# An MoE layer's first and last expert pass: rows by selection matmuls, the router on the unscaled residual

## The chip, the cores and the metric

The kernel runs on one core of one Trainium2 chip. The metric is the time on the device in microseconds (us) for one execution, from three runs. A profile of one execution shows its instructions by engine: TensorE (PE, with the weight loads as PEld), VectorE (DVE), ScalarE (ACT), GpSimd (POOL) and SyncE (SP), and the DMA transfers.

## The reference

A trunk of two layers on 256 tokens of width 1024, all in fp32. Layer 0 is attention with sinks and a dense feed-forward of 3584. Layer 1 is a Mamba2 mixer, then a mixture of eight experts of 3584, two per token. The part that the change touches is the end:

```python
h = h + mix                                   # the mixer's output
hn = rmsnorm(h, ln_ffn[1])
logits = hn @ w_router                        # 256 x 8
top_v, top_i = top_k(logits, 2)
gates = softmax(top_v)
for e in range(8):
    h = h + combine[:, e] * (silu(hn @ w_gate[e]) * (hn @ w_up[e])) @ w_down[e]
return rmsnorm(h, ln_final)
```

`rmsnorm` divides each token's row by the root of its mean square and multiplies by a gain.

## The kernel before

Everything lies in one program with an order written out by hand for each engine, and semaphores between them. Tokens stand in two tiles (`TT` = 2) of 128 partitions: `h` is the residual, `xs` a scratch of the same shape. PSUM is eight banks of 512 columns.

**Weights.** They stream as chunks of 1 MB (128x2048) through a ring of six (`ring`, loaded by SP). For precision every product of the large matrices is made of three matmuls: ScalarE rounds a chunk to `w_hi` (L533 in the expert passes), VectorE computes the rest `w_lo` (L1243), and `product` (L604 to L606) multiplies high by high, high by low and low by high. Three chunks can be split ahead (`SPLIT`); `ahead_e` does it for the chunks that it names, ScalarE once TensorE has used the chunk three before (`chunk_used`), VectorE once `hi_ready` says so. SP refills a ring slot once `lo_ready` counts its chunk.

**Before the passes.** The mixer's out product (L604 to L606 on `yT`) ends; VectorE adds it to `h` (L1251). `norm(3, 24)` follows: ScalarE squares (L377), VectorE and ScalarE make the inverse root (L944 to L954), VectorE scales into `xs` (L962), TensorE transposes (L625), VectorE applies the gain into `hT` (L966), and TensorE makes the router's logits, 16 matmuls with `hT` as weights and eight columns of `rw` (L863). VectorE ranks the logits of each token (L1261 to L1276), TensorE counts how many earlier tokens chose each expert (L869 to L873), VectorE makes gates and slots (up to L1310). A slot is a row of `xg_rows` in HBM: 128 rows for each expert, and 128 more where an expert has over 128 tokens. GpSimd scatters the scaled rows there by four indirect DMAs (L348), ScalarE loads the first expert's 128 rows into `xg` (L554), TensorE transposes them (L882), and ScalarE and VectorE split them into `xgT_hi` (L550) and `xgT_lo` (L1319).

**The passes.** A hardware loop (`Fori`) runs `passes` times, 8 with these inputs, over one expert's 42 chunks: gate and up in `WIDE` = 2, 2, 2, 1 groups of 512 columns (28 chunks; the groups start at chunks 0, 8, 16, 24), then down (14 chunks). The number comes into each engine's register by `value_load`. After a group TensorE transposes the hidden rows (L897), which ScalarE and VectorE split (L562, L1328). Towards the end of gate and up TensorE transposes the next expert's rows. The output, 128 rows in banks 6 and 7, is copied to `yg` (L589) and stored to `y_rows` (L591).

**The tail.** GpSimd waits for all stores and gathers each token's two output rows by four indirect DMAs (L359); VectorE adds them to `h` with the gates (L1361), squares (L1364), makes the inverse root and the scaling (L1370), and SP stores `out` (L302).

What sets the order around the change: each engine's instructions run in the order of its program, so a wait holds all that is behind it on that engine.

## Time and profile before

| | |
|---|---|
| median of 3 runs | 1725.51 us (1725.06 to 1726.12) |
| the profiled execution's own time | 1725.92 us |
| its span, first to last instruction | 1724.2 us |
| mean granted TensorE clock | 0.950 |
| TensorE matmuls busy | 1559.2 us (90%) |
| VectorE busy | 1241.1 us (72%) |
| ScalarE busy | 1043.2 us (61%) |
| GpSimd busy | 43.8 us (3%) |
| TensorE's share of the chain that ended last | 67% |

The span is what the sums below are made against. A busy share is an average over the whole kernel; what a change of one stage is worth is read from the timeline of that stage and from the chain of waits, which is followed back from the last instruction, at each step to what released it. Matmuls are pipelined: a row's length (0.39 us) is longer than the step to the next row (0.23 us), and it is the step that adds up.

### The profile page before, as it was taken

The page shows a single profiled execution, that of the slowest core. Times are in us where ns is not written, and L with a number is a line of the kernel's source. Part 1 is how long each engine was busy: PE and PEld are TensorE (multiplying, and loading weights), DVE is VectorE, ACT ScalarE, POOL GpSimd, SP SyncE. Part 2 cuts the span into 40 slices and gives each one's busy share as a digit, 9 for nine tenths or more (in the row PEclk, how much of TensorE's full clock was granted, in tenths as well). Part 3 has the DMA queues.
Part 4 walks back from the last instruction along what each step waited for, and adds up shares of the span by engine and source line. Part 5 has one row for each costly group of instructions (what it writes and reads, how often), then busy time and mean ns, then how long its engine had stood idle before and what let it go on. Part 6 is the DMA issues. An engine that isn't in the chain of part 4 may idle for free.

```text
span 1724.2 us, 21094 instructions
## 1 busy us (share of the span) xinstructions
PE 1559.2 (90%) x7794; PEld 1304.3 (76%) x7794; DVE 1241.1 (72%) x1045; ACT 1043.2 (61%) x886; POOL 43.8 (3%) x90
## 2 busy tenths in 40 slices
PE   5688999989999895699999999999999999999992
PEld 3566888878899785578778778788777777777781
DVE  4554555445498845488888888788888887887885
ACT  4243444334477642476777777777777777777762
POOL 1004200000000001000000000000000000000000
PEclk8888999998999886799999999999999999999996
DMA  7325955544542332699999999999999999999995
GB/s 247 103 74 202 412 199 187 191 150 147 147 123 98 123 110 81 234 353 371 368 359 375 361 367 370 373 346 381 358 356 387 355 354 386 363 358 374 365 366 193
DMA packets 166402, 477.08 MB, mean 277 GB/s; under 512 B 9105, under 2 KB 34977, under 8 KB 166354
## 3 DMA queue, kind: packets, MB, share of 16 engines
q1 hardware_dynamic: 157682, 446.84, 71.3%
q0 software_dynamic: 5520, 18.05, 2.8%
q10 hardware_dynamic: 3152, 11.54, 1.7%
q8 instruction: 32, 0.52, 0.1%
q14 instruction: 16, 0.13, 0.0%
HBM read 455.42 MB, written 20.97 MB: 276 GB/s over the span
## 4 chain that ended last, share of the span: by engine, by line
PE 67%; DVE 15%; issue 8%; ACT 7%; DMA 2%; DVEq 1%; ACTq 0%; POOL 0%; SPq 0%; POOLq 0%
PE bank L604 21%; PE bank L606 20%; PE bank L605 20%; DVE w_lo L1243 7%; ACT w_hi L533 2%; PE bank L897 1%; DVE acc L1174 1%; DVE w_lo L988 1%; DVE m_hT_lo L1328 1%; ACT m_hT_hi L562 1%; DVE arg L1198 1%; ACT w_hi L392 1%; DVE xgT_lo L1319 1%; DMA ring<-swa_w_qkv_in 1%; PE bank L831 1%
## 5 line engine op out<-in xcount | busy, mean ns | idle before, releaser
L1243 DVE TENSOR_TENSOR w_lo<-ring,w_hi 128x2048 fp32r<-128x2048 f32 x339 | 766.8, 2289 | 117.8 <-ACT w_hi L533 117.8
L533 ACT ACTIVATE w_hi<-ring 128x2048 fp32r<-128x2048 f32 x339 | 648.2, 1919 | 255.9 <-PE bank L606 255.6
L604 PE MATMUL bank<-w_hi,xgT_hi 128*128 128x512 f32 x896 | 355.8, 397 | 23.2 <-DVE w_lo L1243 21.7
L606 PE MATMUL bank<-w_hi,xgT_lo 128*128 128x512 f32 x896 | 350.1, 391 | 0.0
L605 PE MATMUL bank<-w_lo,xgT_hi 128*128 128x512 f32 x896 | 349.9, 391 | 0.0
L988 DVE TENSOR_TENSOR w_lo<-ring,w_hi 128x2048 fp32r<-128x2048 f32 (+1 forms) x84 | 190.0, 2266 | 172.2 <-ACT w_hi L392 171.9
L392 ACT ACTIVATE w_hi<-ring 128x2048 fp32r<-128x2048 f32 (+1 forms) x84 | 159.2, 1898 | 171.9 <-PE bank L606 170.3
L604 PEld LDWEIGHTS bank<-w_hi,xgT_hi 128*128 128x128 f32 x896 | 168.9, 188 | 70.1 <-DVE w_lo L1243 34.8
L606 PEld LDWEIGHTS bank<-w_hi,xgT_lo 128*128 128x128 f32 x896 | 168.8, 188 | 35.9
L605 PEld LDWEIGHTS bank<-w_lo,xgT_hi 128*128 128x128 f32 x896 | 169.1, 189 | 33.4
L604 PE MATMUL bank<-w_hi,m_hT_hi 128*128 128x512 f32 x448 | 176.9, 395 | 3.2 <-DVE w_lo L1243 3.2
L606 PE MATMUL bank<-w_hi,m_hT_lo 128*128 128x512 f32 x448 | 174.6, 390 | 0.0
L605 PE MATMUL bank<-w_lo,m_hT_hi 128*128 128x512 f32 x448 | 174.4, 389 | 0.0
L604 PE MATMUL bank<-w_hi,hT_hi 128*128 128x512 f32 (+1 forms) x336 | 133.1, 396 | 2.9 <-DVE hT_lo L978 2.9
L605 PE MATMUL bank<-w_lo,hT_hi 128*128 128x512 f32 (+1 forms) x336 | 131.6, 392 | 0.0
L606 PE MATMUL bank<-w_hi,hT_lo 128*128 128x512 f32 (+1 forms) x336 | 131.3, 391 | 0.0
L604 PEld LDWEIGHTS bank<-w_hi,m_hT_hi 128*128 128x128 f32 x448 | 84.1, 188 | 23.6 <-DVE w_lo L1243 6.6
L606 PEld LDWEIGHTS bank<-w_hi,m_hT_lo 128*128 128x128 f32 x448 | 84.1, 188 | 17.9
L605 PEld LDWEIGHTS bank<-w_lo,m_hT_hi 128*128 128x128 f32 x448 | 84.2, 188 | 16.5
L604 PEld LDWEIGHTS bank<-w_hi,hT_hi 128*128 128x128 f32 x336 | 64.8, 193 | 18.6 <-DVE hT_lo L978 3.3
L604 PE MATMUL bank<-hT_hi,w_hi 128*128 128x256 f32 x256 | 73.3, 286 | 3.1 <-DVE w_lo L988 1.6
L606 PEld LDWEIGHTS bank<-w_hi,hT_lo 128*128 128x128 f32 x336 | 64.7, 193 | 13.3
(260 smaller groups left out, 1692.1 us busy)
## 6 DMA issues: line engine op xcount, KB each, us to landing
ring<-moe_w_gu_in SPq DMA_DIRECT2D x230, 1024.0 KB, 7.4
ring<-moe_w_down_in SPq DMA_DIRECT2D x112, 1024.0 KB, 7.4
ring<-ffn_w_gu_in SPq DMA_DIRECT2D x28, 1024.0 KB, 5.0
ring<-ffn_w_down_in SPq DMA_DIRECT2D x14, 1024.0 KB, 4.8
xg_rows<-zeros POOLq DMA_DIRECT2D x36, 256.0 KB, 12.5
ring<-ssm_w_in_in SPq DMA_DIRECT2D x8, 1024.0 KB, 4.9
ring<-ssm_w_in_in SPq DMA_DIRECT2D x16, 512.0 KB, 3.8
ring<-ssm_w_in_in SPq DMA_DIRECT2D x32, 256.0 KB, 4.2
```

What stands on the lines that cost most here:

```text
L392: act.activation(w_hi[:, m % SPLIT, 0:w], ring[:, m % RING, 0:w], ACT.Copy).then_inc(hi_ready, 1)
L533: act.activation(w_hi[:, c % SPLIT], ring[:, c % RING], ACT.Copy).then_inc(hi_ready, 1)
L562: act.activation(m_hT_hi[:, 4 * f:4 * f + 4, :], bank[4 + f % 2][:].rearrange("p (a b) -> p a b", b=P), ACT.Copy).then_inc(m_This, 1)
L604: pe.matmul(o, stat[0], mov[0], start=start, stop=False)
L605: pe.matmul(o, stat[0], mov[1], start=False, stop=False)
L606: return pe.matmul(o, stat[1], mov[0], start=False, stop=stop)
L831: ins = pe.matmul(bank[4 + t][:, r * P:(r + 1) * P], dtA[:, t, g * REP + r:g * REP + r + 1].to_broadcast([P, P]), tri[:], start=True, stop ...
L897: ins = pe.transpose(bank[4 + f % 2][:, a * P:(a + 1) * P], m_hh[:, f % 2, a * P:(a + 1) * P], ident[:])
L988: dve.tensor_tensor(w_lo[:, m % SPLIT, 0:w], ring[:, m % RING, 0:w], w_hi[:, m % SPLIT, 0:w].bitcast(F32), ALU.subtract).then_inc(lo_ready, 1)
L1174: ins = dve.scalar_tensor_tensor(acc[:, i], U[:, i, tap:tap + T], cwT[:, tap, ct:ct + 1], acc[:, i], ALU.mult, ALU.add)
L1198: ins = dve.tensor_scalar(arg[:, t, r], bank[4 + t][:, r * P:(r + 1) * P], acol[:, t * SH + g * REP + r:t * SH + g * REP + r + 1], 0.0, AL ...
L1243: dve.tensor_tensor(w_lo[:, c % SPLIT], ring[:, c % RING], w_hi[:, c % SPLIT].bitcast(F32), ALU.subtract).then_inc(lo_ready, 1)
```

## The change

- **Router on the unscaled residual.** The router's weights are multiplied once, early, by the norm's gain (`rwg_ready`). TensorE transposes `h` itself as each half is added; ScalarE copies (`raw_T`); the logits come transposed (8 x 256, `rw` as weights), are copied by ScalarE and transposed back. The ranking needs no scaling. The inverse root `inv` is made from squares on VectorE and used from the selection on; the exponent takes the scaled difference of logits.
- **Residual adds.** Tile 0 of the last out product is finished first, and its adds wait for that alone (`so_first`).
- **Pass 0's rows.** VectorE makes a 128x128 selection for each token tile, one where token and slot of expert 0 meet, times `inv`; 16 fp32 matmuls of `h` by it give the transposed rows in eight PSUM places (`first_rows`); ScalarE and VectorE split them with the gain. Scatter and HBM rows remain for the other passes, and the scatter's preparation (slots, scaled rows `xs`) stands behind that split on VectorE; ScalarE's wait for `rows_ready` is still ahead of its passes. The load of `xg` for the next pass stands in the third group of a pass.
- **Last pass.** The loop runs `last` = passes - 1 times and the last pass is written out behind it. In it VectorE makes the gates (`shares`) and the last expert's selection matrix, gathers for the other outputs run into `xs` (choice 0, then choice 1 once those are added), and VectorE adds them (`rows_added`).
- **Tail.** The last pass's output is not stored; four fp32 matmuls of 512 columns bring its rows back to their tokens, weighted; VectorE adds, ScalarE squares by halves, and `out` is stored in two halves.

```diff
+        first_rows = [bank[b][:, P * a:P * (a + 1)] for b, a in FIRST_AT]
+        sel_first, logits_T = m_sg[:, 0, 0:T].rearrange("p (t s) -> p t s", t=TT), m_sg[0:E, 1, 0:T]
...
+            for t in range(TT):
+                sp.wait_ge(out_ready, t + 1)
+                sp.dma_start(out[0, t * P:(t + 1) * P], xs[:, t]).then_inc(out_stored, 16)
+            sp.wait_ge(out_stored, 16 * TT)
 
 
...
                 pool_e.sem_inc(y_free, 1)
-            for t in range(TT):
-                for i in range(2):
-                    pool_e.indirect_dma_start(y_got[:, i, t], None, y_rows.rearrange("i p d -> (i p) d"),
+
+            for i in range(2):
+                if i == 1:
+                    pool_e.wait_ge(y_added, TT)
+                for t in range(TT):
+                    pool_e.indirect_dma_start(xs[:, t], None, y_rows.rearrange("i p d -> (i p) d"),
                                               bass.IndirectOffsetOnAxis(slots_i[:, i, t:t + 1], 0)
...
+            for i in range(4):
+                act.wait_ge(xT_mm, 12 + i + 1)
+                part = (slice(None), slice((i % 2) * 4, (i % 2) * 4 + 4), slice((i // 2) * P, (i // 2 + 1) * P))
+                act.activation(hT[part], bank[4 + i][:].rearrange("p (a b) -> p a b", b=P), ACT.Copy).then_inc(raw_T, 1)
+            act.wait_ge(var_done, 4)
+            act.activation(st[:, 3, 4:6], st[:, 3, 2:4], ACT.Sqrt).then_inc(sqrt_done, 1)
+            act.wait_ge(r_mm, 1)
+            act.activation(logits_T, bank[0][0:E, 0:T], ACT.Copy).then_inc(r_sb, 1)
+            for k in range(KD):
+                act.wait_ge(first_mm, (1, 1, 2, 2, 3, 3, 4, 5)[k])
+                act.activation(xgT_hi[:, k], first_rows[k], ACT.Copy,
+                               scale=vT[:, 24 + k:25 + k]).then_inc(first_hi, 1)
+            ahead_e(0, 2, AHEAD)
             act.wait_ge(r_max, 1)
             act.activation(rt[:, 2], rt[:, 1], ACT.Exp).then_inc(r_exp, 1)
             act.wait_ge(rows_ready, TT)
             act.dma_start(gain_row, ln_final.partition_broadcast(P)).then_inc(gain_loaded, 16)
-            ahead_e(0, 2, AHEAD)
             act.wait_ge(r_passes, 1)
-            passes = act.value_load(passes_i[0:1, 0:1], min_val=E, max_val=2 * E)
-
-            def rows_split(at):
...
+                    act.activation(sel_last_T, bank[0][:, 0:T].rearrange("p (t s) -> p t s", t=TT), ACT.Copy
+                                   ).then_inc(last_sb, 1)
+                else:
...
+                    load_roots(4)
+                    act.wait_ge(m_y, it + 1)
+                    act.wait_ge(y_free, it + 1)
+                    act.activation(yg[:, 0:512], bank[6][:], ACT.Copy).then_inc(y_left, 1)
+                    return
...
-                act.wait_ge(slot_loaded[r], passes * (LAYER_CHUNKS // RING * 16) + (slot_base[r] + 16))
-            act.wait_ge(xg_loaded, passes * 16 + 32)
-            load_roots(4)
+
+            with act.Fori(0, last) as it:
+                expert(it, False)
+            expert(last, True)
+            for n in range(2):
+                for t in range(TT):
+                    act.wait_ge(h_final, 2 * n + t + 1)
+                    act.activation(xs[:, t, 512 * n:512 * (n + 1)], h[:, t, 512 * n:512 * (n + 1)], ACT.Square,
+                                   accum_out=rt[:, 12, 2 * n + t:2 * n + t + 1]).then_inc(sq_final, 1)
+            for r in range(RING):
+                act.wait_ge(slot_loaded[r], last * (LAYER_CHUNKS // RING * 16)
+                            + (slot_base[r] + LAYER_CHUNKS // RING * 16 + 16))
             act.wait_ge(var_done, 5)
...
+            out_product(7, (0,)).then_inc(so_first, 1)
+            out_product(7, (1,))
+
+
...
+                    if k % 4 == 0:
+                        pe.wait_ge(h_done, 8 + 2 * t + k // 4 + 1)
+                    ins = pe.transpose(bank[4 + 2 * t + k // 4][:, (k % 4) * P:(k % 4 + 1) * P],
+                                       h[:, t, k * P:(k + 1) * P], ident[:])
+                    if k % 4 == 3:
+                        ins.then_inc(xT_mm, 1)
+            pe.wait_ge(rwg_ready, 1)
+            for t in range(TT):
+                for k in range(KD):
+                    if k % 4 == 0:
+                        pe.wait_ge(raw_T, 2 * t + k // 4 + 1)
+                    ins = pe.matmul(bank[0][0:E, t * P:(t + 1) * P], rw[:, k, :], hT[:, k, t * P:(t + 1) * P],
                                     start=(k == 0), stop=(k == KD - 1))
+            ins.then_inc(r_mm, 1)
+            pe.wait_ge(r_sb, 1)
+            for t in range(TT):
+                ins = pe.transpose(bank[0][:, T + t * E:T + (t + 1) * E], logits_T[:, t * P:(t + 1) * P],
+                                   ident[0:E, 0:E])
             ins.then_inc(r_logit, 1)
             pe.wait_ge(r_sel, 1)
             chosen = rt[:, 5].rearrange("p (t e) -> p t e", t=TT)
 
             pe.matmul(bank[1][:, 0:E], tri_lt[:], chosen[:, 0, :], start=True, stop=True)
             pe.matmul(bank[1][:, E:2 * E], ones[:], chosen[:, 0, :], start=True, stop=False)
...
-            pe.matmul(bank[1][:, 2 * E:3 * E], ones[:], chosen[:, 0, :], start=True, stop=False)
-            pe.matmul(bank[1][:, 2 * E:3 * E], ones[:], chosen[:, 1, :], start=False, stop=True).then_inc(r_cnt, 1)
+            pe.matmul(bank[1][:, E:2 * E], tri_lt[:], chosen[:, 1, :], start=False, stop=True).then_inc(r_cnt, 1)
...
+
+            pe.wait_ge(sel_ready, 1)
+            for k in range(KD):
+                for t in range(TT):
+                    ins = pe.matmul(first_rows[k], h[:, t, k * P:(k + 1) * P], sel_first[:, t],
+                                    start=(t == 0), stop=(t == TT - 1))
+                if FIRST_AT[k] not in ((2, 0), (3, 0), (4, 0)):
+                    ins.then_inc(first_mm, 1)
             pe.wait_ge(r_passes, 1)
-            passes = pe.value_load(passes_i[0:1, 0:1], min_val=E, max_val=2 * E)
-
-
-            def rows_transposed(at):
-
-                pe.wait_ge(xg_loaded, at * 16 + 16)
+            last = pe.value_load(last_i[0:1, 0:1], min_val=E - 1, max_val=2 * E - 1)
...
                             m_transposes(2 * j - 1)
                 pe.wait_ge(m_silu, it * NJ + NJ)
-                rows_transposed(it + 1)
+                if is_last:
+                    pe.wait_ge(last_ready, 1)
+                    for t in range(TT):
+                        ins = pe.transpose(bank[0][:, t * P:(t + 1) * P], sel_last[:, t], ident[:])
+                    ins.then_inc(last_T, 1)
+                else:
+                    rows_transposed(it)
...
+            with pe.Fori(0, last) as it:
+                expert(it, False)
+            expert(last, True)
+
+            pe.wait_ge(last_sb, 1)
+            for n in range(2):
+                pe.wait_ge((y_left, y_right)[n], 1)
+                for t in range(TT):
+                    pe.matmul(bank[2 * n + t][:], sel_last_T[:, t], yg[:, 512 * n:512 * (n + 1)], start=True,
+                              stop=True).then_inc(back_mm, 1)
...
+            for t in range(TT):
+                dve.wait_ge(*((so_first, 1), (chunk_used, SO0 + KI // 2))[t])
                 for n in range(2):
...
+            dve.drain()
+            for t in range(TT):
+                dve.scalar_tensor_tensor(xs[:, t], h[:, t], 1.0, h[:, t], ALU.mult, ALU.mult,
+                                         accum_out=st[:, 3, t:t + 1])
+            dve.drain()
+            variance(D, st[:, 3], var_done)
...
+            inv = inverse(st[:, 3], sqrt_done, 4)
+            dve.tensor_reduce(rt[:, 7, 0:TT], r3[0], AXX, ALU.max)
+
+            place = bank[1][:, 0:2 * E].rearrange("p (t e) -> p t e", t=TT)
+            dve.wait_ge(column_ready, 1)
+            dve.wait_ge(r_cnt, 1)
+            dve.scalar_tensor_tensor(rt[:, 11, 0:TT], r3[5][:, :, 0], -FAR, place[:, :, 0], ALU.mult, ALU.add)
+            dve.drain()
+            for t in range(TT):
+                ins = dve.tensor_scalar(sel_first[:, t], column, rt[:, 11, t:t + 1], inv[:, t:t + 1], ALU.is_equal,
+                                        ALU.mult)
+            ins.then_inc(sel_ready, 1)
+            dve.wait_ge(r_cnt, 2)
+            dve.tensor_reduce(rt[:, 9, 0:1], bank[0][:, 0:E], AXX, ALU.max)
+            dve.tensor_scalar(r3[6], place, P - 0.5, float((E - 1) * P), ALU.is_gt, ALU.mult)
+            dve.drain()
+            dve.tensor_scalar(rt[:, 9, 1:2], rt[:, 9, 0:1], P + 0.5, float(E), ALU.is_gt, ALU.mult)
+            dve.tensor_tensor(r3[6], r3[6], first_slot[:], ALU.add)
+            dve.drain()
+            dve.tensor_scalar(last_i[:], rt[:, 9, 1:2], float(E - 1), None, ALU.add).then_inc(r_passes, 1)
+            dve.tensor_tensor(r3[6], r3[6], place, ALU.add)
+
+
+            for k in range(KD):
+                dve.wait_ge(first_hi, (2, 2, 4, 4, 6, 6, 7, 8)[k])
+                ins = dve.scalar_tensor_tensor(xgT_lo[:, k], first_rows[k], vT[:, 24 + k:25 + k],
+                                               xgT_hi[:, k].bitcast(F32), ALU.mult, ALU.subtract)
+                if k % 4 == 3:
+                    ins.then_inc(xg_lo, 1)
+            ahead_e(0, 2, AHEAD)
...
+            dve.tensor_tensor(r3[1], r3[0], rt[:, 7, 0:TT].unsqueeze(2).to_broadcast([P, TT, E]), ALU.subtract)
...
+            dve.drain()
+            dve.tensor_tensor(r3[1], r3[1], inv.unsqueeze(2).to_broadcast([P, TT, E]), ALU.mult).then_inc(r_max, 1)
             dve.tensor_tensor(by_choice[:], choice[:], r3[6].unsqueeze(1).to_broadcast([P, 2, TT, E]), ALU.mult)
             dve.drain()
             dve.tensor_reduce(slots[:], by_choice[:], AXX, ALU.add)
             dve.drain()
             dve.tensor_copy(slots_i[:], slots[:]).then_inc(r_slots, 1)
-            ahead_e(0, 2, AHEAD)
+            dve.wait_ge(ffn_gain_loaded, 16)
+            for t in range(TT):
+                dve.scalar_tensor_tensor(xs[:, t], h[:, t], inv[:, t:t + 1], gain_row, ALU.mult,
+                                         ALU.mult).then_inc(rows_ready, 1)
...
+            def shares():
+
+                dve.wait_ge(r_exp, 1)
...
+                for t in range(TT):
+                    ins = dve.tensor_scalar(sel_last[:, t], column, rt[:, 14, t:t + 1], rt[:, 13, t:t + 1],
+                                            ALU.is_equal, ALU.mult)
+                ins.then_inc(last_ready, 1)
+
+            def rows_added(i, t):
+
+                dve.wait_ge(y_got_in, 16 * TT * (i + 1))
+                dve.scalar_tensor_tensor(h[:, t], xs[:, t], gates[:, i, t:t + 1], h[:, t], ALU.mult,
+                                         ALU.add).then_inc(y_added, 1)
...
+                    if is_last and j == 0:
+                        shares()
+                    if is_last and j == 2:
+                        rows_added(0, 0)
+                    ahead_e(it, up + 3, up + wide + 3)
+                    if is_last and j == 2:
+                        rows_added(0, 1)
+                    ahead_e(it, up + wide + 3, up + 2 * wide + 3)
...
-                rows_split(it + 1)
+                if not is_last:
+                    rows_split(it)
...
+                ahead_e(it, c + 4, c + 6)
+                if is_last:
+                    rows_added(1, 0)
+                ahead_e(it, c + 6, c + 8)
+                if is_last:
+                    rows_added(1, 1)
+                ahead_e(it, c + 8, LAYER_CHUNKS)
+                if not is_last:
+                    ahead_e(it + 1, 0, AHEAD)
+
+            with dve.Fori(0, last) as it:
+                expert(it, False)
+            expert(last, True)
+            dve.wait_ge(chunk_used, last * LAYER_CHUNKS + (MOE0 + LAYER_CHUNKS))
+            dve.tensor_copy(yg[:, 512:1024], bank[7][:]).then_inc(y_right, 1)
+            for n in range(2):
                 for t in range(TT):
-                    dve.wait_ge(y_got_in, 16 * 2 * TT)
-                    dve.scalar_tensor_tensor(h[:, t], y_got[:, i, t], gates[:, i, t:t + 1], h[:, t], ALU.mult, ALU.add)
-                dve.drain()
-            for t in range(TT):
-                dve.scalar_tensor_tensor(xs[:, t], h[:, t], 1.0, h[:, t], ALU.mult, ALU.mult,
-                                         accum_out=st[:, 4, t:t + 1])
+                    dve.wait_ge(back_mm, 2 * n + t + 1)
+                    hh = h[:, t, 512 * n:512 * (n + 1)]
+                    dve.tensor_tensor(hh, hh, bank[2 * n + t][:], ALU.add).then_inc(h_final, 1)
+            dve.wait_ge(sq_final, 4)
+            dve.tensor_tensor(st[:, 4, 0:2], rt[:, 12, 0:2], rt[:, 12, 2:4], ALU.add)
```

## Rows read from the trace of the kernel before

**Rows 1.** Timeline: start and length in us, engine, line, operation; before the passes.
```profile
654.78 2.29 DVE L1243 TENSOR_TENSOR w_lo<-ring,w_hi 128x2048 fp32r<-128x2048 f32 x1 [2.47 <-ACT w_hi L533]
...
657.78 0.39 PE L606 MATMUL bank<-w_hi,yT_lo 128*128 128x512 f32 x1
658.21 2.73 DVE L1251 SCALAR_TENSOR_TENSOR h<-bank,st,h 128x512 f32<-128x512 f32 x4 [1.14 <-PE bank L606]
...
669.05 7.00 PE L863 MATMUL bank<-rw,hT 128*128 128x8 f32 x32 [0.78 <-DVE hT L966]
...
678.07 0.18 DVE L1276 TENSOR_SCALAR rt<-rt 128x16 f32<-128x16 f32 x1
...
705.09 0.79 PE L604 MATMUL bank<-w_hi,xgT_hi 128*128 128x512 f32 x1 [1.49 <-DVE xgT_lo L1319]
```

**Rows 2.** Chain of waits: start and length in us, what; passes 0 and 1.
```profile
688.24 10.11 DMA xg_rows<-xs,slots_i
...
705.88 0.43 PE bank L605
...
727.45 0.50 PE bank L604
727.95 0.23 PE bank L605
...
918.49 1.29 DVE xgT_lo L1319 x2
```

**Rows 3.** Timeline of the end of the last pass and the tail.
```profile
1691.24 0.39 PE L606 MATMUL bank<-w_hi,m_hT_lo 128*128 128x512 f32 x1
...
1708.08 5.04 DVE L1361 SCALAR_TENSOR_TENSOR h<-y_got,gates,h 128x1024 f32<-128x1024 f32 x4 [12.18 <-DMA y_got<-y_rows,slots_i]
...
1715.68 0.17 DVE L944 TENSOR_SCALAR st<-st 128x2 f32<-128x2 f32 x1
...
1717.32 2.48 DVE L1370 SCALAR_TENSOR_TENSOR xs<-h,st,gain_row 128x1024 f32<-128x1024 f32 x2
1719.83 0.39 SPq L302 DMA_DIRECT2D out<-xs  x1
```

**Rows 4.** Timelines of TensorE, VectorE and ScalarE, start of pass 1.
```profile
839.11 0.50 PE L604 MATMUL bank<-w_hi,xgT_hi 128*128 128x512 f32 x1 [1.41 <-DVE w_lo L1243]
...
850.68 0.50 PE L604 MATMUL bank<-w_hi,xgT_hi 128*128 128x512 f32 x1 [0.38 <-DVE w_lo L1243]
...
848.34 6.70 DVE L1243 TENSOR_TENSOR w_lo<-ring,w_hi 128x2048 fp32r<-128x2048 f32 x3 [1.91 <-ACT w_hi L533]
...
844.12 1.28 ACT L572 ACT_TABLE_LOAD   x1
```

**Rows 5.** Timeline of TensorE in the scan stage: fp32 matmuls.
```profile
545.61 2.00 PE L831 MATMUL bank<-tri,dts 128*128 128x128 f32 x16
...
547.89 0.60 PE L844 MATMUL bank<-xs 128*128 128x256 f32 x2
548.33 0.38 PE L845 MATMUL bank<-xs 128*128 128x128 f32 x2
```

**Rows 6.** Stretches: busy us and count per engine, PEclk, DMA share, GB/s.
```profile
658.00:664.00 6.00, 0.17 (x1) 0.00 (x0) 3.93 (x11) 3.78 (x6) 0.00 (x0) 0.92 0.00 0
...
850.00:973.00 123.00, 119.73 (x541) 97.92 (x540) 104.12 (x59) 91.12 (x63) 0.00 (x0) 1.00 0.99 366
```

**Rows 7.** Source line 544: instructions, ns min/median/max, first and last start.
```profile
L544 ACTq TENSOR_LOAD <-passes_i x1: 469/469/469, 681.5 to 681.5; - x1
```

**Rows 8.** The page, part 5: groups, busy us, mean ns, idle before.
```profile
L1243 DVE TENSOR_TENSOR w_lo<-ring,w_hi 128x2048 fp32r<-128x2048 f32 x339 | 766.8, 2289 | 117.8 <-ACT w_hi L533 117.8
L533 ACT ACTIVATE w_hi<-ring 128x2048 fp32r<-128x2048 f32 x339 | 648.2, 1919 | 255.9 <-PE bank L606 255.6
```

**Rows 9.** Source lines 338 and 348: the DMA issues of POOL, ns.
```profile
L338 POOL DMA_DIRECT2D xg_rows<-zeros x36: 542/543/584, 153.5 to 172.2; - x36
...
L348 POOL DMA_INDIRECT xg_rows<-xs,slots_i x4: 955/975/2189, 683.2 to 688.2; - x4
```

131 lines of the change are left out of this document (64 added, 67 removed).

## The prediction

> **What bounds the kernel now.** I read the page's chain first: most of it is TensorE in the split matmuls of the expert passes, which run one behind the other. The change does not touch these, nor the splitting of the weights. So I looked for where TensorE stands still around them, and two stretches come out. In the timeline of the stretch before the passes, the out product's last matmul starts at 657.78 and ends 0.39 later, at 658.17, and the first matmul of pass 0 starts at 705.09 [rows 1]: 46.9 us. The chain of waits fills them: 2.7 of residual adds, squares, a root, transposes, 7.0 of router matmuls, the ranking, then the scatter (10.11 from its last issue to landing) and the load of `xg` [rows 1, 2]. After the last matmul, which starts at 1691.24 and ends at 1691.6, come 32.6 us to the end of the span at 1724.2 [rows 3]: the store of `yg`, four gathers, four adds (5.0), squares, root, scaling, the store of `out`. Between them lie eight passes; pass 0 reaches its chunk 7 at 727.45, pass 1 at 850.68 [rows 2, 4], 123.2 us apart. All eight look alike, so a gain in front is worth what it moves the arrival at chunk 7 of pass 0, and a gain behind is worth what it takes off the 32.6.
>
> **The front, up to the first expert matmul.** Z is 658.17.
> Residual adds: 2.73 for four [rows 1]. The first two now wait only for the half product of tile 0, but VectorE is busy with a `w_lo` until 657.07 [rows 1], so they run 657.1 to 658.5 and the others to 659.9: 1.1 us earlier, not 2.7. Transposes of `h` follow each add; with four at 0.5 (four records of 0.125, [rows 5]) they end at 660.4. The norm's root goes off the path: two squares on VectorE of 1.26 each (as an add of that size, [rows 3]) end at 662.4, the root is needed only at the selection. The matmul now has `rw` as weights and 128 token columns, 16 of fp32, 32 records. The nearest rows are 16 records of fp32 128x128 in 2.00 us at full clock [rows 5], and the 32 of the old router in 7.00 at half [rows 1, 6]; so 4.0 or 7.0, less if the eight-column weights load quickly. I take 3.6 (full clock, since TensorE has been nearly continuously busy since Z): 664.0. Then a copy of 256 columns (an estimate from the 0.68 of a 512-column add: 0.4), two transposes and hops, 0.9: 664.9. The ranking took from 676.05, the router's end, to 678.25 [rows 1], with one instruction more: 667.0. Three of five count matmuls at 0.44 (two records of 0.22, [rows 1]) end at 668.4; meanwhile VectorE makes the inverse root (1.2 of the tail's 1.64, [rows 3]) and the maximum, 668.4; offset 0.25 and two 128x128 selections of 0.3 each (an estimate, under half the 0.68 of 512 columns): 669.2.
> The selection: 16 fp32 matmuls, 32 records, 4.0 us at full clock and 7.0 at half [rows 1, 5]. Over 658 to 664 the mean clock was 0.92 with TensorE idle [rows 6]: 1.00 for 5 us, then 0.50, so it fell 4.9 us after Z; here it stands nearly idle from 664.9 to 669.2 with only the counts between. I take mostly half clock with a rise near the end: 6.2, so 675.4. The last `xgT_hi` (estimated 0.35 for 128 columns), the last `xgT_lo` (0.3) and hops are 0.85, and TensorE's own load of `last` costs 0.5 and some registers, about the same [rows 7]. First expert matmul S = 676.4, against 705.09: 28.7 earlier, between 27.5 (all half clock) and 31 (all full).
>
> **What is late next: the scatter's instructions now stand in the first chunks' way.** The pass has three chunks split ahead and needs chunk 3 at S + 8.2 (12 matmuls of 0.227 per chunk, 2.72, at full clock, [rows 2]). Before, VectorE and ScalarE had all else done while the scatter ran. After, VectorE does, behind the last `xgT_lo`: the `w_lo` of chunk 2 (its `w_hi`, 1.92, [rows 8], starts after the last `first_hi`, so S + 1.4 to S + 3.7), some seven small instructions for exponent and slots (1.2), the two scaled rows of 1.2 each: `rows_ready` at S + 7.4. ScalarE waits for `rows_ready` ahead of a DMA issue (0.33), its load of `last` and registers (0.47, and 0.5 estimated, [rows 7]), then the loop's table load (1.28, [rows 4]) and the `w_hi` of chunk 3 (1.92); then `w_lo` (2.29) [rows 8]: S + 14.4. TensorE idles from S + 8.2, 6.2 us. A 4.9 us idle lost the clock after Z [rows 6], so chunk 3 runs at 0.427 per matmul, as pass 0 began before [rows 2]: 2.3 more. From chunk 3 to chunk 7 pass 1 took 11.57, from 839.11 to 850.68, through `w_hi`, a table load, two `silu` and `w_hi` [rows 4]; that chain starts at chunk 3's end. So chunk 7 comes at S + 14.4 + 11.6 + 2.3 = S + 28.3 = 704.7, against 727.45 (S + 22.4 before, [rows 2]). The front's gain at chunk 7 is 22.7: 28.7 earned, 6.0 given back. Ends: 16 if the entry costs twice what I think, 31 if chunk 3 is in time and all is at full clock.
>
> **In the passes.** The scatter runs beside pass 0. POOL's four issues began from 683.2 to 688.2, and the last landed 10.11 later, 15 us after the first began [rows 2, 9]; from S + 8.5 that is S + 24, and the load of `xg` that waits for it stands at ScalarE's third group, past S + 47. Weights use 0.99 of the DMA time at 366 GB/s in a pass [rows 6], but `w_lo` waited for ScalarE alone, in all 117.8 us [rows 8], and while it idles to S + 14.4 nothing asks for chunk 9. Zero. The moved `xg` issue stands where ScalarE's next `w_hi` ends over 1 us before VectorE wants it: zero, at most 0.35 x 7.
> Last pass: the dozen small instructions of `shares` (2.2) fall into VectorE's 1.9 idle before chunk 7's `w_lo` [rows 4]: 0.3. Of four `rows_added` at 1.26 [rows 3], the first stands right on the chain `m_hT_lo`, `w_lo`, TensorE: 1.3, the second 0.3, the two in the down part have 0.4 idle per chunk and 1.1 of lead: 0. Removed are the two `xgT_lo`, together 1.29, from the chain [rows 2] and six transposes (0.7): -1.9. Sum 0, between -2 and +6. The gathers for choice 0 are issued 10 us into the pass and wanted at 47 us; those for choice 1 are issued after the adds and wanted about 40 us later.
>
> **The tail.** T is the last matmul's end, 1691.6. The left half of `yg` is copied 0.6 before T, the right half by VectorE until T + 0.7. Four fp32 matmuls of 512 columns: a 256-column one and its successor are 0.44 apart [rows 5], so 0.88 each, 3.5 in all at full clock; the halves overlap with the adds (0.68 each), last add T + 4.3, last square on ScalarE (0.6 + 0.2) T + 5.1, sum and drain 0.3, then as before from 1715.68 to 1719.80 the root and two scalings, 4.1 [rows 3]: T + 9.6. The `out` store took 4.4 from 1719.83; of its half I take 3.9. T + 13.5 against T + 32.6: 19.1 gained, between 16 (matmuls at half clock) and 20.
>
> **The Trainium skill against this.** POOL's 36 zero-fill issues stood beside VectorE's work of the dense stage, `w_lo` among it, and took 542 to 584 ns each [rows 9]; no blocking shows in them. The Trainium skill, page "SBUF — State Buffer", section "Who interferes with whom" and the box on the "DVE blocks DMA" trap, says GpSimd and VectorE share a port pair that one of them holds exclusively, and descriptors of POOL's DMAs are not written meanwhile; "GPSIMD Engine Reference", "Key points", adds VectorE instructions with two SBUF inputs, which `w_lo` is. This would put the scatter and gathers, which stood in idle stretches, under the lock. By that rule the time is the third rival's below.
>
> **The sum.** 1724.2 - 22.7 - 19.1 + 0 = 1682.4 for the span. The median of the runs (1725.5) is 1.3 above this span, and the profiled run itself 1725.9, 1.7 above: 1684 by the median.
>
> **The rivals.**
> 1. Entry is not late: ScalarE's wait for `rows_ready` or the small instructions are hidden, chunk 3 starts by S + 9, and no clock is lost: 5.5 to 8 less, 1677. For it: only three chunks lie ahead, and I have sized the VectorE queue from single rows. Against: the order is written out, and `rows_ready` is behind 2.3 + 1.2 + 2.4 of it. Chance 0.17.
> 2. Longer hops and half clock all the way through the router too (3.4 more), with a later entry (3 more): 1691. For it: pass 0 began at half clock before [rows 2]. Chance 0.12.
> 3. The change runs its indirect DMAs beside `w_lo`, and each takes VectorE's time: eight issues of 0.97 [rows 9], fully on VectorE's critical stretches, 8 us: 1692. Chance 0.06.
> 4. Slower than before: the gathers of the last pass starve behind the weight stream (0.99 DMA share, [rows 6]). VectorE waits for them in order, with `w_lo` behind it, and so TensorE. The first pair is wanted 37 us after its issue, landing took 10 for the scatter's [rows 2]; from 37 us on, each microsecond counts once, and beyond about 79 us the kernel is slower than before; at 85 us it takes 1732. Against: the scatter landed in 10 while three weight loads were in flight with it. Chance 0.02.
> 5. The change does not do what it says, since the expert loads would fill more than 128 rows and passes exceed 8: excluded by the 339 `w_lo`, 8 x 42 and three ahead [rows 8].
>
> **How the numbers follow.** The forecast, 1684 with its own range 1679 to 1689, has 0.62. The range goes from 1676 (rival 1 with a full-clock front) to 1693 (rival 3), leaving out about 0.15. Measurement tells 0.2% from no change, 3.5 us; every case but rival 4 is faster by ten times that: faster 0.97, same 0.01, slower 0.02.
>
> **What would show it.** First expert matmul 18 us after Z; a TensorE gap of some 6 us before chunk 3 ending in `w_lo`, with ScalarE's table load before it; chunk 7 some 28 us into the pass; passes 123 us apart; the last pass within 2 us of the others; 13.5 us from the last expert matmul to the end. Wrong if the gap before chunk 3 is absent (rival 1) or over 9 us, if `w_lo` grows beyond 2.3 us, or if VectorE waits for a gather.

## The result and the profile after

The changed kernel takes 1681.58 us (median of 4 runs, 1680.24 to 1683.25) against 1725.82 for the kernel before it in the same runs (1725.06 to 1726.12): ratio 0.9745, 95% interval 0.9728 to 0.9762, so 44.2 us less. Its profiled execution has a span of 1681.5 us. The forecast was 1684.

The timeline of the changed kernel from the out product's last matmul to chunk 7 of pass 0 (start and length in us, engine, line, operation; in brackets the idle time before and what ended it); it answers to [rows 1, 2]:

```profile
658.43 2.72 DVE L1344 SCALAR_TENSOR_TENSOR h<-bank,st,h 128x512 f32<-128x512 f32 x4
659.23 0.39 PE L651 MATMUL bank<-w_hi,yT_lo 128*128 128x512 f32 x1
661.79 3.66 PE L919 MATMUL bank<-hT,rw 128*8 128x128 f32 x32
668.15 0.17 DVE L1370 TENSOR_SCALAR rt<-rt 128x16 f32<-128x16 f32 x1
670.18 0.60 DVE L1380 TENSOR_SCALAR m_sg<-trig,rt,st 128x128 f32<-128x128 f32 x2
670.83 5.62 PE L940 MATMUL bank<-m_sg,h 128*128 128x128 f32 x32
677.51 0.49 PE L649 MATMUL bank<-w_hi,xgT_hi 128*128 128x512 f32 x1 [1.06 <-DVE xgT_lo L1396]
...
681.99 2.47 DVE L1415 SCALAR_TENSOR_TENSOR xs<-h,st,gain_row 128x1024 f32<-128x1024 f32 x2
684.49 0.33 ACTq L570 DMA_DIRECT2D gain_row<-ln_final_in  x1
685.91 1.28 ACT L549 ACT_TABLE_LOAD   x1 [4.19 <-issue]
687.21 5.51 ACT L549 ACTIVATE w_hi<-ring 128x2048 fp32r<-128x2048 f32 x3
691.49 0.80 PE L649 MATMUL bank<-w_hi,xgT_hi 128*128 128x512 f32 x1 [5.51 <-DVE w_lo L1336]
```

Z, the end of the out product, is 659.62. The router takes 3.66 on a TensorE that has not rested; ranking and counts come back; the selection runs from 670.83; the first expert matmul is S = 677.51 = Z + 17.9 (before: Z + 46.9). Then comes the price: ScalarE waits for the scaled rows (681.99 to 684.46), issues the load of the gain row, loads `last`, loads a table, and only at 687.21 makes the `w_hi` of chunk 3. TensorE idles 5.51 us and starts chunk 3 at 691.49; chunk 7 follows at 704.70, Z + 45.1 (before: Z + 69.3).

The clock in that stretch (us, then busy time and count of TensorE, its weight loads, VectorE, ScalarE and GpSimd, then PEclk, DMA share, GB/s):

```profile
666.00:668.00 2.00, 0.20 (x2) 0.11 (x2) 1.46 (x6) 0.00 (x0) 0.00 (x0) 0.94 0.00 0
668.00:670.00 2.00, 1.62 (x8) 1.62 (x8) 1.20 (x9) 0.00 (x0) 0.00 (x0) 0.50 0.00 0
...
690.00:694.00 4.00, 2.51 (x6) 2.04 (x7) 4.00 (x3) 2.72 (x2) 2.27 (x1) 0.50 0.65 181
```

The granted clock falls to 0.50 (1.2 GHz) twice: where TensorE waits for the ranking, and in the wait for chunk 3.

The timeline of the last pass and the tail of the changed kernel, answering to [rows 3]:

```profile
1565.78 0.50 PE L649 MATMUL bank<-w_hi,xgT_hi 128*128 128x512 f32 x1 [0.48 <-DVE w_lo L1336]
...
1614.09 0.50 PE L649 MATMUL bank<-w_hi,xgT_hi 128*128 128x512 f32 x1 [1.77 <-DVE w_lo L1336]
...
1668.04 0.60 ACT L619 ACTIVATE yg<-bank 128x512 f32<-128x512 f32 x1 [4.08 <-PE bank L651]
1668.79 3.67 PE L1019 MATMUL bank<-yg,zeros 128*128 128x512 f32 x8
...
1675.93 2.48 DVE L1520 SCALAR_TENSOR_TENSOR xs<-h,st,gain_row 128x1024 f32<-128x1024 f32 x2
1677.24 1.55 SPq L313 DMA_DIRECT2D out<-xs  x2
```

T, the last expert matmul's end, is 1668.69, and the end comes 12.8 us later (before: 32.6).

The changed kernel and all kernels made from it have the same program up to Z (the kernel before lacks the early product of router weights and gain, the new order at the end of the out product and some small preparations), and yet Z lies between 656.5 and 659.6 in their profiles. So I compare traces from Z on. From Z to the end the kernel before takes 1724.2 - 658.17 = 1066.0, the changed one 1021.9: 44.1 less, of it 24.2 up to chunk 7 of pass 0, 0.2 from there to T, 19.8 behind T.

### The profile page after: what moved, and what is told of

Its sections match the earlier page's. It is cut to its first block, busy times and chain, and to the rows that moved or that the text cites. A ratio compares the mean times of both kernels' runs of the same rounds, so it can differ in the third digit from the quotient of the medians.

```text
span 1681.5 us, 21145 instructions
## 1 busy us (share of the span) xinstructions
PE 1562.1 (93%) x7822; PEld 1302.9 (77%) x7822; DVE 1233.8 (73%) x1056; ACT 1037.6 (62%) x894; POOL 56.9 (3%) x93
## 4 chain that ended last, share of the span: by engine, by line
PE 69%; DVE 15%; issue 7%; ACT 7%; DVEq 1%; DMA 1%; ACTq 1%; SPq 0%
PE bank L649 21%; PE bank L651 21%; PE bank L650 20%; DVE w_lo L1336 7%; ACT w_hi L549 2%; PE bank L964 1%; DVE acc L1267 1%; DVE w_lo L1079 1%; DVE m_hT_lo L1459 1%; ACT m_hT_hi L586 1%; DVE arg L1291 1%; ACT w_hi L408 1%; DMA ring<-swa_w_qkv_in 1%; PE bank L877 1%; DVE xgT_lo L1452 1%
## 5 line engine op out<-in xcount | busy, mean ns | idle before, releaser
L1336 DVE TENSOR_TENSOR w_lo<-ring,w_hi 128x2048 fp32r<-128x2048 f32 x336 | 759.6, 2288 | 110.5 <-ACT w_hi L549 110.4
L651 PEld LDWEIGHTS bank<-w_hi,m_hT_lo 128*128 128x128 f32 x448 | 84.1, 188 | 17.9
```

The costliest lines, as they stand in the source:

```text
L651: return pe.matmul(o, stat[1], mov[0], start=False, stop=stop)
L1336: dve.tensor_tensor(w_lo[:, c % SPLIT], ring[:, c % RING], w_hi[:, c % SPLIT].bitcast(F32), ALU.subtract).then_inc(lo_ready, 1)
```

## The experiments

All edits are to the changed kernel. The first three columns are the median, its ratio to the kernel before and the 95% interval; the others, from each profile, are: from Z to the end, to the first expert matmul, to chunk 3 and to chunk 7 of pass 0; from that chunk 7 to T; from T to the end. The rows stem from four sets of runs, each with the kernel before in it (medians 1725.4 to 1725.8); the changed kernel was timed in the first set alone, so small differences between medians are read with the trace beside them.

| kernel | us | ratio | interval | Z to end | S | chunk 3 | chunk 7 | to T | tail |
|---|---|---|---|---|---|---|---|---|---|
| before | 1725.8 | 1 | | 1066.0 | 46.9 | 57.9 | 69.3 | 964.2 | 32.6 |
| changed | 1681.6 | 0.9745 | .9728-.9762 | 1021.9 | 17.9 | 31.9 | 45.1 | 964.0 | 12.8 |
| e6 tail undone | 1697.4 | 0.9838 | .9821-.9854 | 1036.7 | 18.0 | 31.9 | 45.2 | 961.5 | 30.0 |
| e7 router scaled | 1692.3 | 0.9797 | .9776-.9817 | 1031.5 | 26.9 | 41.1 | 54.8 | 963.9 | 12.8 |
| e8 selection undone | 1696.4 | 0.9828 | .9812-.9845 | 1036.1 | 37.4 | 48.0 | 59.4 | 963.9 | 12.8 |
| e1 gain moved | 1678.3 | 0.9730 | .9717-.9743 | 1018.5 | 17.9 | 28.6 | 41.7 | 964.0 | 12.8 |
| e2 exponent early | 1675.4 | 0.9704 | .9691-.9717 | 1014.4 | 18.0 | 26.2 | 37.7 | 963.9 | 12.8 |
| e3 entry clear | 1675.1 | 0.9710 | .9697-.9723 | 1014.5 | 17.9 | 26.2 | 37.7 | 964.0 | 12.8 |
| e4 rows on GpSimd | 1676.1 | 0.9711 | .9698-.9725 | 1016.1 | 19.0 | 27.3 | 39.5 | 963.7 | 12.9 |
| e5 warm | 1681.1 | 0.9743 | .9727-.9760 | 1020.4 | 15.7 | 29.7 | 43.7 | 963.9 | 12.9 |
| e10 small gathers | 1682.0 | 0.9744 | .9730-.9757 | 1021.9 | 17.9 | 31.9 | 45.1 | 964.0 | 12.8 |
| e9 two loads | 1683.4 | 0.9752 | .9739-.9766 | 1024.6 | 17.9 | 31.9 | 45.2 | 966.7 | 12.8 |
| e12 together | 1671.6 | 0.9684 | .9671-.9697 | 1010.9 | 15.7 | 24.0 | 35.5 | 962.6 | 12.8 |
| e13 Silu first | 1666.1 | 0.9651 | .9638-.9664 | 1005.8 | 15.7 | 24.0 | 34.9 | 958.0 | 12.9 |

**Each part undone by itself.** First the tail.

```diff
-                if is_last:
-                    load_roots(4)
...
-                    act.activation(yg[:, 0:512], bank[6][:], ACT.Copy).then_inc(y_left, 1)
-                    return
...
-                    pe.matmul(bank[2 * n + t][:], sel_last_T[:, t], yg[:, 512 * n:512 * (n + 1)], start=True,
-                              stop=True).then_inc(back_mm, 1)
...
+            pool_e.wait_ge(y_stored, last * 16 + 16)
...
+                    pool_e.indirect_dma_start(y_got[:, i, t], None, y_rows.rearrange("i p d -> (i p) d"),
...
+                    dve.scalar_tensor_tensor(h[:, t], y_got[:, i, t], gates[:, i, t:t + 1], h[:, t], ALU.mult, ALU.add)
```

> Edit to the changed kernel: front and written-out last pass stay, but the last pass stores its outputs, all four gathers follow it, and the adds, squares, root and store of out are those of the kernel before. Theory A (the tail's gain is the round trip through DRAM): 32.6 us from the last expert matmul to the end instead of 12.8; the last pass is 0.9 shorter between its chunk 7 and its end since the adds no longer stand in it; the pass ahead of it stays at 121.9 us, since the two table loads of the loop are gone with the writing out, not with the new tail: 1681.6 + 19.8 - 0.9 = 1700.5. Rival B (the 1.3 us of the last pass are the tail's doing): 1701.8. Rival C (the store of yg and the gathers are faster here than before, since fewer loads stand beside them): under 1698.

Measured: 1697.4, 15.9 more, and 14.8 in the trace: 17.2 more behind T, 2.5 less between chunk 7 and T. The tail is 30.0, not 32.6. Theories A and B did not have that; rival C had the time (under 1698), but gave as its cause a faster store and faster gathers. The timeline of the kernel before where `yg` is copied, and below it that of e6, with its first adds:

```profile
1691.67 1.91 ACT L533 ACTIVATE w_hi<-ring 128x2048 fp32r<-128x2048 f32 x1 [0.80 <-PE bank L606]
1693.48 1.07 ACT L589 ACTIVATE yg<-bank 128x512 f32<-128x512 f32 x2
```

```profile
1662.53 1.28 ACT L617 ACTIVATE yg<-bank 128x512 f32<-128x512 f32 x2 [5.56 <-PE bank L638]
...
1676.81 2.48 DVE L1469 SCALAR_TENSOR_TENSOR h<-y_got,gates,h 128x1024 f32<-128x1024 f32 x2 [17.50 <-DMA y_got<-y_rows,slots_i]
```

Before, ScalarE still split a chunk of a next pass that never came, and copied `yg` from T + 1.9; written out, the last pass has no next one, and the copy starts at T - 0.7. From the copy's start to the first add it is 14.6 before and 14.3 in e6, so rival C's cause is worth 0.3 at most. So 2.5 of the tail's 19.8 come from writing the pass out, 17.2 from the matmuls that return its outputs.

Then the router on the normalised rows again:

```diff
+            inv = inverse(st[:, 3], sqrt_done, 4)
+            for t in range(TT):
+                dve.tensor_scalar(xs[:, t, :], h[:, t, :], inv[:, t:t + 1], None, ALU.mult).then_inc(xs_done, 1)
...
-                                       h[:, t, k * P:(k + 1) * P], ident[:])
+                                       xs[:, t, k * P:(k + 1) * P], ident[:])
```

> Edit to the changed kernel: the router sees the normalised rows again (squares, root, scaling, then transposes), the selection matmuls and the tail stay. Theory A (the norm's chain comes onto the path and TensorE idles in it and loses the clock): router starts at Z + 8.0 instead of Z + 2.2, takes 7.0 instead of 3.7, the inverse root after the ranking is gone (0.3 on the path, since the counts take as long): first expert matmul at Z + 26.5 instead of Z + 17.9, 8.6 us more: 1690. Rival B (the clock is not lost in the wait): 3.3 less than that, 1687.

Transposes and router in e7's timeline:

```profile
665.35 3.67 PE L910 MATMUL bank<-ident,xs 128*128 128x128 f32 x16 [6.53 <-DVE xs L1354]
668.95 4.40 PE L919 MATMUL bank<-hT,rw 128*8 128x128 f32 x32
```

TensorE waits 6.53 us for the norm, and transposes and router take 3.67 and 4.40 instead of 2.41 and 3.66. S is 9.0 later and chunk 7 9.7: theory A's total, but not its terms. The router began at Z + 10.1, not Z + 8.0, and ran at half clock for a small part only; transposes and router together lost 2.0 where A had 3.3 for the router alone. The four runs spread from 1686.5 to 1693.2, so the trace is the better measure here.

Pass 0's rows through scatter and gather again:

```diff
-                    ins = pe.matmul(first_rows[k], h[:, t, k * P:(k + 1) * P], sel_first[:, t],
-                                    start=(t == 0), stop=(t == TT - 1))
...
+            act.dma_start(xg, xg_rows[0]).then_inc(rows_back, 16)
...
+            pe.wait_ge(rows_back, 16)
...
+                ins = pe.transpose(bank[k // 4][:, (k % 4) * P:(k % 4 + 1) * P], xg[:, k * P:(k + 1) * P], ident[:])
```

> Edit to the changed kernel: pass 0's rows go through the scatter and a load of xg again, transposed and split as in the kernel before; the router on the unscaled residual and the tail stay. Theory A: slots and scaled rows at Z + 15.8, four scatter issues 5.2, landing about 10, load of xg 2.5, transposes and split 2.5: first expert matmul at Z + 36.5 instead of Z + 17.9; but the entry is clear again (chunk 7 at S + 22.4 instead of S + 27.2), so chunk 7 at Z + 58.9 instead of Z + 45.1: 13.8 us more, 1695.4. Rival B (the late chunk 3 is no property of the selection's short stretch and stays): 18.6 more, 1700.

The transposes of `xg` in e8's timeline:

```profile
692.12 1.97 PE L943 MATMUL bank<-ident,xg 128*128 128x128 f32 x8 [22.90 <-DMA xg<-xg_rows]
```

TensorE waited 22.90 us for that load. S is at Z + 37.4 and chunk 7 at Z + 59.4, so S + 22.0 against S + 27.2 in the changed kernel: theory A. The selection earns 19.5 at S and keeps 14.3 at chunk 7. In the traces the three parts are worth 14.8, 9.6 and 14.2 from Z to the end. What the written-out pass is worth by itself is e6 against the kernel before, from chunk 7 of pass 0 to the end: 991.5 against 996.8, so 5.3. The sum is 43.9 of 44.1. The earlier adds of tile 0, kept in all of these kernels, were not undone by themselves.

**The entry of pass 0.** The three kernels take one thing after another out of the wait for chunk 3. First e1:

```diff
-            act.wait_ge(rows_ready, TT)
-            act.dma_start(gain_row, ln_final.partition_broadcast(P)).then_inc(gain_loaded, 16)
...
+                    if is_last and j == 1:
+                        act.wait_ge(rows_ready, TT)
+                        act.dma_start(gain_row, ln_final.partition_broadcast(P)).then_inc(gain_loaded, 16)
```

> Edit to the changed kernel: ScalarE's wait for rows_ready and the load of the last gain row (the DMA issue behind it) move out of the entry of pass 0 into the written-out last pass. Theory A (ScalarE's wait holds chunk 3 and the long idle costs the clock): the w_hi of chunk 3 starts about 184.4-Z style, that is 24.8 us after the end Z of the out product instead of 27.6, its w_lo ends at Z + 29.0; TensorE idles 2.5 us instead of 5.5, the clock stays up and chunk 3's matmuls take 0.23 instead of 0.43: 3.0 + 2.3 = 5.3 us less, 1676.3. Rival B (VectorE is the late one: its w_lo of chunk 2, small instructions, scaled rows and its load of last fill the same time): idle stays above 4 us, at most 1.5 less, 1680 to 1681.6. Rival C (the clock is lost for another reason than this idle stretch): 3.0 less only, 1678.6.

The `w_hi` of chunk 3 and TensorE's chunk 3 in e1's timeline, and e1's stretch behind:

```profile
681.12 5.51 ACT L549 ACTIVATE w_hi<-ring 128x2048 fp32r<-128x2048 f32 x3
...
685.42 0.69 PE L650 MATMUL bank<-w_hi,xgT_hi 128*128 128x512 f32 x1 [2.19 <-DVE w_lo L1337]
```

```profile
685.00:689.00 4.00, 3.58 (x9) 2.80 (x10) 4.00 (x3) 1.64 (x1) 3.39 (x3) 0.57 0.72 174
```

The wait for `rows_ready` was what held ScalarE: the idle stretch is 2.19 instead of 5.51. But the clock falls all the same, to 0.57 in the mean of 685 to 689: theory A's second half is wrong, and 3.4 is gained, not 5.3. That is rival C's number (1678.6), though e2 shows that the clock does depend on this idle stretch: one of 2.19 us was still long enough to lose it here. Next, e2:

```diff
             act.activation(logits_T, bank[0][0:E, 0:T], ACT.Copy).then_inc(r_sb, 1)
+            act.activation(root_table[:, 4:5], ones[:, 4:5], ACT.Exp)
+            act.wait_ge(r_max, 1)
+            act.activation(rt[:, 2], rt[:, 1], ACT.Exp).then_inc(r_exp, 1)
...
             dve.tensor_tensor(r3[6], r3[6], place, ALU.add)
+            dve.drain()
+            dve.tensor_tensor(r3[1], r3[0], rt[:, 7, 0:TT].unsqueeze(2).to_broadcast([P, TT, E]), ALU.subtract)
...
+            dve.tensor_copy(slots_i[:], slots[:]).then_inc(r_slots, 1)
```

> As e1_gain_moved, and the ranking's small instructions (choice, slots, the exponent's argument) move into VectorE's idle stretch between the offset and the first xgT_lo, ScalarE's Exp and its table load to between the logits' copy and the first xgT_hi. Theory A: VectorE has 1.2 us less ahead of the w_lo of chunk 3 and ScalarE 1.6 + 1.3 less; VectorE is now the one that binds: w_lo of chunk 2 until Z + 21.4, scaled rows 2.5, its load of last about 1, w_lo 2.3: chunk 3 at Z + 27.3, idle 1.2 us, 1.3 to 1.7 less than e1_gain_moved, 1674.8. Rival B (ScalarE waits for r_max longer than its stretch allows, and the xgT_hi start late): S up to 1 us later, no gain over e1_gain_moved, 1676.3 to 1677.

The timelines of ScalarE, VectorE and TensorE in e2:

```profile
678.71 1.28 ACT L549 ACT_TABLE_LOAD   x1
680.58 1.92 ACT L549 ACTIVATE w_hi<-ring 128x2048 fp32r<-128x2048 f32 x1 [0.59 <-PE bank L653]
...
683.33 4.49 DVE L1338 TENSOR_TENSOR w_lo<-ring,w_hi 128x2048 fp32r<-128x2048 f32 x2
...
685.83 0.39 PE L651 MATMUL bank<-w_hi,xgT_hi 128*128 128x512 f32 x1
```

ScalarE is now ready at 680.58, VectorE's `w_lo` ends at 685.6, and TensorE goes on at 685.83 without a gap, at full clock: chunk 7 at Z + 37.7, 7.4 earlier than in the changed kernel and 6.2 less by the medians. With the last 2.2 of idle the clock's loss went too.

e3 moves the loads of `last` as well, and e4 makes the scaled rows on GpSimd:

> As e2_exp_early, and the loads of last on VectorE and ScalarE move into the same idle stretches ahead of the selection's results. Theory A: 1 us less on VectorE's queue ahead of the w_lo of chunk 3: chunk 3 at Z + 26.4, idle 0.3 us, 0.9 less than e2_exp_early, 1673.9. Rival B (the load of last on ScalarE delays the Exp and with it the first xgT_hi): S later by 0.5 to 1 us and the same time as e2_exp_early, 1674.8.

```diff
-                dve.scalar_tensor_tensor(xs[:, t], h[:, t], inv[:, t:t + 1], gain_row, ALU.mult,
-                                         ALU.mult).then_inc(rows_ready, 1)
...
+                pool_e.tensor_scalar(xs[:, t], h[:, t], st[:, 3, 6 + t:7 + t], None, ALU.mult)
...
+                pool_e.tensor_tensor(xs[:, t], xs[:, t], gain_row, ALU.mult).then_inc(rows_ready, 1)
```

> As e3_entry_clear, and the two scaled rows are made by GpSimd (two plain instructions for each instead of VectorE's one). Theory A (VectorE's queue alone still held chunk 3): chunk 3 is in time, no idle stretch ahead of it, 0.3 to 1 us less than e3_entry_clear, 1673.3; the scatter starts later, and nobody waits for it. Rival B (GpSimd's elementwise instructions with two SBUF inputs and VectorE's w_lo or small instructions take turns at the SBUF): w_lo of chunks 2 and 3 or the xgT_lo grow by some tenths to microseconds, and the time is 1 to 5 us longer than e3_entry_clear. Rival C (the scatter ends too late for the load of xg in pass 0): a TensorE idle stretch ahead of the transposes of xg, more than 5 us longer.

e3 equals e2 in the trace, since the entry was clear already: the 0.9 of its theory A did not come. e4 is worse by 1.5 there, 1.0 by the medians. Its timelines show GpSimd's two steps of the scaling, and VectorE's instructions of 16 columns and `w_lo` beside them:

```profile
669.78 5.68 POOL L360 TENSOR_SCALAR xs<-h,st 128x1024 f32<-128x1024 f32 x2 [487.32 <-DVE m_sg L1389]
669.94 0.98 DVE L1397 TENSOR_TENSOR rt<-rt,first_slot 128x16 f32<-128x16 f32 x1
672.75 1.00 DVE L1406 TENSOR_TENSOR rt<-rt,st 128x16 f32<-128x16 f32 x1
...
680.53 6.82 POOL L363 TENSOR_TENSOR xs<-xs,gain_row 128x1024 f32<-128x1024 f32 x2 [5.07 <-issue]
682.46 11.44 DVE L1345 TENSOR_TENSOR w_lo<-ring,w_hi 128x2048 fp32r<-128x2048 f32 x4 [2.27 <-ACT w_hi L556]
```

The first of the two small ones takes 0.17 in e2 and 0.98 here, while GpSimd's scaling runs, and S came 1.1 later. The `w_lo` grow too: of the four in the last row the first takes 2.63 and the second, of chunk 4, 4.32 instead of 2.29, and TensorE waits 0.92 us for it. GpSimd's multiplication by the gain row takes 2.41 and then 4.45, so both sides lose. That is rival B as it was written down.

**The clock in the selection.**

```diff
+            for _ in range(8):
+                pe.matmul(bank[7][:, 0:P], ident[:], hT[:, 0, 0:P], start=True, stop=True)
             pe.wait_ge(r_sel, 1)
...
+            for _ in range(4):
+                pe.matmul(bank[7][:, 0:P], ident[:], hT[:, 0, 0:P], start=True, stop=True)
             pe.wait_ge(sel_ready, 1)
```

> Edit to the changed kernel: 8 fp32 matmuls of 128 columns into a free bank while TensorE waits for the ranking, 4 while it waits for the selection. Theory A (the clock falls because TensorE stands idle for 2.2 us there, and the selection is slow for that alone): the granted clock stays at 1.00 from Z to the first expert matmul, the counts take 0.22 instead of 0.43 each and the selection 4.1 instead of 5.4: first expert matmul at Z + 16.0 instead of Z + 17.9, 1.9 us less, 1679.7. Rival B (the counts of 8 columns are no work that holds the clock, and it falls in them): up to 0.6 less, 1681. Rival C (the extra matmuls end later than the ranking and stand in the way): 0.5 to 1 us more.

Stretches of e5, and below them the selection in its timeline:

```profile
666.00:668.00 2.00, 1.80 (x16) 1.61 (x16) 1.48 (x10) 0.00 (x0) 0.00 (x0) 1.00 0.00 0
...
690.00:694.00 4.00, 4.00 (x12) 3.12 (x11) 2.01 (x1) 0.81 (x1) 0.00 (x0) 0.56 0.95 347
```

```profile
668.85 3.76 PE L944 MATMUL bank<-m_sg,h 128*128 128x128 f32 x32
```

The clock stays at 1.00 up to S, the selection takes 3.76 instead of 5.62, S is 2.2 earlier: theory A up to there. But the 5.5 us of idle ahead of chunk 3 stay, TensorE starts again at 687.67 and the clock is back only about 693.5, so chunk 3 takes 5.3 instead of 4.5. Chunk 7 is 1.4 earlier, and the medians, 0.5 apart, do not resolve it.

**GpSimd beside VectorE.** 24 more gathers of 8 KB beside the `w_lo` of pass 0:

```diff
+            for c in range(10, 34):
+                pool_e.wait_ge(hi_ready, MOE0 + c + 1)
+                pool_e.indirect_dma_start(zeros[:, 16 * (c - 10):16 * (c - 9)], None, xg_rows.rearrange("i p (a d) -> (i p a) d", d=16),
```

> Edit to the changed kernel: GpSimd issues 24 more indirect gathers of 128 rows of 64 bytes (8 KB each, so hardly any traffic) beside the w_lo of pass 0, each paced by a w_hi. Theory A (GpSimd waits for VectorE and not the other way round): GpSimd's issues take 2 to 5 us beside w_lo instead of 0.95 alone, w_lo stays within 0.1 of 2.29, and the time is the same, up to 0.5 more: 1681.6 to 1682.1. Rival B (each issue takes VectorE's time, as my third rival had it): 24 x 0.95, 23 us more at most and at least 10, w_lo of pass 0 near 3.2: 1692 to 1705.

Timelines of GpSimd and VectorE and the page's group of `w_lo` in e10:

```profile
710.15 3.08 POOL L368 DMA_INDIRECT zeros<-xg_rows,slots_i  x1 [0.30 <-issue]
...
717.58 2.29 DVE L1343 TENSOR_TENSOR w_lo<-ring,w_hi 128x2048 fp32r<-128x2048 f32 x1 [0.42 <-ACT w_hi L556]
718.27 2.42 POOL L368 DMA_INDIRECT zeros<-xg_rows,slots_i  x1 [0.30 <-issue]
...
733.64 4.60 DVE L1343 TENSOR_TENSOR w_lo<-ring,w_hi 128x2048 fp32r<-128x2048 f32 x2
733.65 0.95 POOL L368 DMA_INDIRECT zeros<-xg_rows,slots_i  x1 [0.30 <-issue]
```

```profile
L1343 DVE TENSOR_TENSOR w_lo<-ring,w_hi 128x2048 fp32r<-128x2048 f32 x336 | 759.7, 2288 | 110.4 <-ACT w_hi L556 110.3
```

The issues take 0.94 to 3.08 us, `w_lo` stays at 2288 ns in the mean, and time and trace are the changed kernel's (1021.9 from Z both): theory A. The rows show how: each of the 18 issues that began while a `w_lo` was under way ended 0.8 to 0.9 us after the end of that `w_lo` (718.27 + 2.42 against 717.58 + 2.29), so one that began early in it took long. Two began within 0.01 us of a `w_lo`'s start (733.65 is one); they took 0.95, and that `w_lo` 2.33. No `w_lo` took over 2.35, and the four issues that met none took 0.94 or 0.95. So GpSimd waits for VectorE here, and nobody waits for GpSimd.

**The table loads of the last pass.** (`load_roots` is one Sqrt of one column.) In the last pass chunk 3 has no gap, and chunk 7 comes 1565.78 - 1443.90 = 121.9 after that of pass 6, against 123.2 before. The row of pass 6:

```profile
1443.90 0.50 PE L649 MATMUL bank<-w_hi,xgT_hi 128*128 128x512 f32 x1 [0.38 <-DVE w_lo L1336]
```

```diff
             def expert(it, is_last):
+                if is_last:
+                    load_roots(4)
```

> Edit to the changed kernel: one Sqrt of one column at the start of the written-out last pass, so that this pass has the two table loads that the loop body has. Theory A (the last pass is 1.3 us shorter from chunk 7 to chunk 7 only because straight-line code keeps the Silu table): a TensorE gap of 1.35 to 1.55 ahead of chunk 3 of the last pass, chunk 7 to chunk 7 is 123.2 instead of 121.9, 1.3 more: 1682.9. Rival B (the last pass is shorter since the registers and branches of the loop are gone): 121.9 stays and the time is 1681.6.

Timelines of ScalarE and TensorE at the start of e9's last pass:

```profile
1547.21 1.28 ACT L386 ACT_TABLE_LOAD   x1 [0.68 <-ACT yg L629]
...
1552.90 0.50 PE L652 MATMUL bank<-w_hi,xgT_hi 128*128 128x512 f32 x1 [1.12 <-DVE w_lo L1339]
1564.60 0.50 PE L652 MATMUL bank<-w_hi,xgT_hi 128*128 128x512 f32 x1 [0.48 <-DVE w_lo L1339]
```

The gap ahead of chunk 3 is back (1.12), and chunk 7 to chunk 7 is 123.2 again: theory A. The medians differ by 1.8. The trace has 2.7 more, since another 1.3 went after the gap of 1.77 at the adds: in e9 the clock fell there (0.50 over 1614.8 to 1616.8), in the changed kernel's profile the same gap left it at 1.00.

**Put together.** e12 has e2's cleared entry (small instructions now in VectorE's wait for the `w_hi` of chunk 2, Exp behind that `w_hi`), e5's matmuls, and in the last pass all four gathers at once, the second pair into `hT`:

```diff
                 ahead_e(it, c + 4, c + 6)
                 if is_last:
-                    rows_added(1, 0)
+                    rows_added(0, 0)
                 ahead_e(it, c + 6, c + 8)
                 if is_last:
-                    rows_added(1, 1)
+                    rows_added(0, 1)
                 ahead_e(it, c + 8, LAYER_CHUNKS)
+                if is_last:
+                    dve.drain()
+                    rows_added(1, 0)
+                    rows_added(1, 1)
```

> The version that should beat both: the changed kernel with the entry cleared (gain row's load in the last pass, small instructions ahead of VectorE's wait for the w_hi of chunk 2, Exp behind that w_hi, its table loaded early), the 12 matmuls that hold the clock, and in the last pass all four gathers issued at once (the second pair into hT, which is free) with the first two adds in the down part and the last two behind the last w_lo. Theory A (the three gains add, since the entry no longer stalls and so the clock that the selection keeps isn't lost again): chunk 7 at Z + 35.5 instead of Z + 45.1 (7.4 from the entry, 2.2 from the clock), the stall of 1.77 us in the last pass back to 0.57: 9.6 + 1.2 less, 1670.8. Rival B (what the clock gives in front is given back behind, as e5_warm gave back 0.8 of 2.2 in chunk 3): 1671.6 to 1673. Rival C (the adds behind the last w_lo end after TensorE's last matmul and delay the tail): up to 2.5 more.

In the table: chunk 7 at Z + 35.5 as theory A says, chunk 7 to T 1.4 less; 1671.6, the expected 1670.8 within the interval. The median alone would also fit rival B (1671.6 to 1673); the trace does not, with chunk 7 at 35.5 against e2's 37.7. So e5's 2.2 are kept in full once there is no idle stretch behind them. e13 adds one instruction to the loop body:

```diff
             def expert(it, is_last):
+                if not is_last:
+                    act.activation(root_table[:, 4:5], ones[:, 4:5], ACT.Silu)
```

> As e12_together, and the loop body of the passes begins on ScalarE with one Silu of one column, so that its first table load is Silu's and the second one, ahead of the first Silu of m_sg, is not needed. Theory A (the table loads that a loop body pays are on the path of the w_hi and so of TensorE, which is where the last pass of the changed kernel won its 1.3 us): the gap ahead of chunk 3 stays at 1.35 to 1.6 us (the first load stays, and 0.2 is added), the 0.38 ahead of chunk 7 goes and perhaps parts of the 0.57 ones behind it: 7 x 0.2 to 0.4, 1.4 to 2.8 less, 1668.7. Rival B (only the load at the top of the body is on the path): no gain, or up to 7 x 0.2 = 1.4 more for the added instruction.

ScalarE's timeline at the start of a pass, first of the changed kernel, then of e13:

```profile
810.85 1.28 ACT L549 ACT_TABLE_LOAD   x1 [1.04 <-issue]
...
821.43 1.28 ACT L596 ACT_TABLE_LOAD   x1
822.73 1.09 ACT L596 ACTIVATE m_sg<-bank 128x512 f32<-128x512 f32 x2
```

```profile
1410.00 1.28 ACT L584 ACT_TABLE_LOAD   x1 [0.90 <-ACT yg L631]
...
1420.56 1.06 ACT L601 ACTIVATE m_sg<-bank 128x512 f32<-128x512 f32 x2
```

The second load is gone, the gap ahead of chunk 7 with it, and each of the seven looped passes is about 0.7 us shorter: 5.1 from Z to the end, 5.5 by the medians, more than theory A gave it. 1666.1 is 0.9908 of the changed kernel.

## Why the prediction was right, and where it was not

**The front's steps.** From Z, predicted and measured: adds end 1.7 and 1.5, router ends 5.8 and 5.8, logits back 6.7 and 6.6, ranking 8.8 and 8.7, selection ready 11.0 and 11.2, selection ended 17.2 and 16.8, S 18.2 and 17.9. The guess between half and full clock for the selection (6.2) was 0.6 too much: 5.62. The prices came from rows of like instructions, and the only choice of weight was the clock. For the clock I had one case to go by, a loss after 4.9 us of idle; e1's idle stretch of 2.19 lost it too.

**What is late next.** The order of the queue was right: ScalarE behind `rows_ready`, then the issue, the load of `last`, the table and `w_hi`. Chunk 3 was foreseen at S + 14.4 (the terms that I named add up to 14.2) and came at S + 14.0; chunk 7 at S + 28.3 and came at S + 27.2. Against the S + 22.4 of before that gives back 4.8, where I had 6.0; the front gave 24.2, not 22.7. e1 and e2 show that this was a real cost and not a bound set by something else. Against a clear entry it is more, 7.4: my measure, the kernel before, had begun its first pass at half clock itself. Rival 1 (1677) describes e2's kernel, which takes 1675.4, and not this one. Rival 2 would be a longer way to S: it did not come.

**The passes.** The sum 0 was nearly right (chunk 7 of pass 6 to T: 225.2 before, 224.8 after) and its terms were not; that they came out so close is luck. The step that failed is the term for what is removed, two `xgT_lo` and six transposes, at -1.9 (1.29 and 0.7 would be 2.0). In e6, which has them removed and no adds, the rest of the pass from the third gap on is 0.7 shorter, not 1.9, so most of their time must have lain beside other work (argued, no run takes them out alone). `shares` cost about 0.8 (I had 0.3), the adds 1.5 (I had 1.6). What made up for it was a term I did not have: straight-line code keeps the Silu table. In e6, where nothing else stands in that stretch, the pass is 1.4 shorter ahead of chunk 3 and 0.7 at chunks 7 and 8; e9 puts the tables back with `shares` in place and costs 1.3. So -0.7, +0.8, +1.5 and -2.1 make the 0.5 by which the last pass is shorter (122.8 against 123.3 from its first matmul to T). The table load of a pass stood in my own rows [rows 4], and I took it as given for a written-out pass too.

**The tail.** 13.5 foreseen, 12.8 measured; the difference is in the store of `out`, which ends 3.1 after the last scaling (1678.41 to 1681.5) where I had 3.9. The early copy of `yg` was in my sum, but I had put all of the gain down to the matmuls; e6 gives 2.5 of the 19.8 to the written-out pass.

**GpSimd.** The third rival had the collision and the wrong side paying. GpSimd's timeline in the last pass of the changed kernel:

```profile
1617.70 4.95 POOL L375 DMA_INDIRECT xs<-y_rows,slots_i  x1 [55.44 <-DVE h L1445]
1622.95 5.29 POOL L375 DMA_INDIRECT xs<-y_rows,slots_i  x1 [0.30 <-issue]
```

These two gather issues, beside `w_lo`, take 4.95 and 5.29 us, and the scatter's last issue 3.05, where an issue takes about 0.97 alone; one of 2.19 stood in the old rows already [rows 9]. e10 shows that `w_lo` pays next to nothing, 0.05 us for an issue that began with it. The Trainium skill, page "SBUF — State Buffer", section "Who interferes with whom", calls the shared port pair an exclusive lock and says that the order of issue decides who blocks. The issues and `w_lo` of e10 agree with that. The same section of the Trainium skill takes `tensor_tensor` to leave DMAs alone, since a probe did not see it stall them, and that page's box on the "DVE blocks DMA" trap speaks of VectorE's perf-mode instructions only. Here the traces differ: `w_lo` is a plain `tensor_tensor`, and the indirect issues wait for its end (up to 3.08 in e10 against 0.95). The 36 direct zero-fill issues in the prediction's [rows 9], of which about a third lay wholly beside a `w_lo`, were not slowed (542 to 584 ns), so what holds for indirect issues does not hold for all of GpSimd's. For GpSimd's elementwise instructions e4 shows VectorE paying as well (0.17 to 0.98, and 2.29 to 4.32 for a `w_lo`).

**Table loads.** The runs show two loads of 1.28 us in each looped pass, none in the straight-line one until the root's near its end, and one when the body begins with a Silu. The Trainium skill, page "ScalarE activation tables: per-element evaluation and per-set limits", section "Table sets in the compiler and the runtime", says that the loads are placed per block; that agrees, and it is the rule that would have given me the missing term.

**Rival 4**, gathers that starve, did not come: VectorE waited for none of them, and they landed 9.7 to 12.1 us after their issue.

## What to carry to other kernels

When a long wait is taken away, list what each engine had been doing inside it, since that work now stands in the next stage's way: here it cost 7.4 of 29.0 us, and moving it into the shorter waits that remained gave it back. Here a gain that hung on the clock was partly lost in the idle stretch behind it (e5, 1.4 of 2.2 left at chunk 7) and kept without that stretch (e12), so clear the stalls first and warm the engine second. And ask of every loop body which ScalarE table it begins and ends with.

## What the runs showed of the hardware that I had not expected

- The clock after an idle stretch: gaps of 1.34 to 1.41 us in every looped pass and of 0.92 in e4 left it at 1.00; the one of 1.77 in the last pass left it at 1.00 in nine profiles and was followed by 0.50 in e9's; one of 2.19 (e1), after which work had already begun again, brought it to 0.50. Counted from the last matmul's end, the fall came after 4.9 us in the kernel before, 2.3 in the changed one ahead of chunk 3, 2.3 in e1 and 4.5 in e5. After the 5.5 us of idle it was back 3.6 us after the restart in the changed kernel, 5.8 us after it in e5. What decides this stays open; no run here tells it apart.
- GpSimd and VectorE: an indirect DMA issue of 0.95 us takes up to 5.29 beside `w_lo`, which stays at 2.29 (2.33 to 2.35 where the issue began first); a VectorE instruction of 0.17 takes up to 1.00 and a `w_lo` up to 4.32 beside GpSimd's elementwise instructions of 1024 columns.
- Programs that are equal up to there reach the same point up to 3 us apart (Z from 656.5 to 659.6); comparing traces from a common point takes that out.
